# Second feed-forward of a fused decoder layer: a weight slot and two weight sums moved ahead of the last norms, the last rows' gain and bias moved from GpSimd to VectorE, and buffers of their own for two groups' sums

## What is computed

```python
x = _layernorm(ALPHA * x + m, ln2_g, ln2_b)                      # m: the mixer's output times w_out
x = _layernorm(ALPHA * x + 0.5 * _swiglu(x, w_gate, w_up, w_down), ln3_g, ln3_b)
```

## Time and profile before

| | us |
|---|---|
| median of 3 runs | 2378.47 |
| lowest, highest | 2376.24, 2378.83 |
| the profiled execution's own time | 2370.88 |
| its span, first to last instruction | 2368.3 |

### The profile page before, as it was taken

How to read it: one execution, slowest core, us unless ns; L and a number is a source line. 1 busy time by engine, 2 the same in 40 slices (tenths; PEclk the granted TensorE clock), 3 DMA queues, 4 the chain that set the end, 5 groups by cost and what they waited for, 6 DMA issues and landing times.

```text
span 2368.3 us, 52206 instructions
## 1 busy us (share of the span) xinstructions
PE 2281.4 (96%) x21030; PEld 2022.1 (85%) x21030; DVE 1563.6 (66%) x2616; ACT 1025.5 (43%) x1839; POOL 457.8 (19%) x452
## 2 busy tenths in 40 slices
PE   7999999999999999999998999997999999999997
PEld 7999999988888788856567898786999999998886
DVE  6776766665686756766644666747777766675577
ACT  6333333355454747544543353524433333345442
POOL 4222200001025102101110132446223300000105
PEclk9999999999999999999999999998999999999999
DMA  4465532378555444533332122434455533349652
GB/s 165 145 220 193 189 104 84 121 246 279 184 185 184 126 121 110 153 71 81 72 83 106 44 71 72 166 117 153 156 192 186 198 127 112 104 148 329 200 176 108
DMA packets 322577, 348.28 MB, mean 147 GB/s; under 512 B 49921, under 2 KB 220754, under 8 KB 321570
## 3 DMA queue, kind: packets, MB, share of 16 engines
q1 hardware_dynamic: 259650, 286.40, 38.1%
q10 hardware_dynamic: 60576, 53.65, 6.7%
q0 software_dynamic: 2112, 4.89, 0.8%
HBM read 245.91 MB, written 98.44 MB: 145 GB/s over the span
## 4 chain that ended last, share of the span: by engine, by line
PE 79%; DVE 9%; issue 5%; ACT 4%; DMA 1%; POOL 1%; SPq 1%; ACTq 0%; POOLq 0%; DVEq 0%
PE ps_b L763 19%; PE ps_a L763 18%; PE ps_a L470 7%; PE ps_b L470 6%; PE ps_pj L1541 4%; PE ps_rk L3253 4%; PE ps_wo L4075 4%; PE ps_mp L2306 2%; PE ps_pj L1523 2%; PE ps_mp L2334 2%; PE ps_rk L3349 1%; PE ps_mp L2320 1%; PE ps_rk L3263 1%; PE ps_mp L2288 1%; PE ps_rk L3401 1%
## 5 line engine op out<-in xcount | busy, mean ns | idle before, releaser
L763 PE MATMUL ps_b<-X_b,W_b 128*128 128x272 f32 x3696 | 466.7, 289 | 8.9 <-DVE X_b L1036 7.8
L763 PEld LDWEIGHTS ps_b<-X_b,W_b 128*128 128x128 f32 x3696 | 465.2, 189 | 10.3 <-DVE X_b L1036 8.0
L763 PE MATMUL ps_a<-X_a,W_a 128*128 128x272 f32 x3696 | 466.7, 289 | 5.6 <-DVE X_a L1036 2.4
L763 PEld LDWEIGHTS ps_a<-X_a,W_a 128*128 128x128 f32 x3696 | 464.9, 189 | 7.5 <-DVE G_a L1093 3.4
L470 PE MATMUL ps_b<-W_b,H_b 128*128 128x512 f32 x924 | 214.8, 389 | 1.0 <-DVE H_b L1122 1.0
L470 PE MATMUL ps_a<-W_a,H_a 128*128 128x512 f32 x924 | 215.3, 389 | 0.0
L470 PEld LDWEIGHTS ps_b<-W_b,H_b 128*128 128x128 f32 x924 | 173.3, 188 | 37.4 <-DVE W_b L1075 1.4
L470 PEld LDWEIGHTS ps_a<-W_a,H_a 128*128 128x128 f32 x924 | 173.2, 188 | 35.8
L844 ACT ACTIVATE W_b<-wraw_b 128x512 fp32r<-128x512 f32 x154 | 95.8, 629 | 164.2 <-PE ps_b L763 64.3
L844 ACT ACTIVATE W_a<-wraw_a 128x512 fp32r<-128x512 f32 x154 | 95.8, 629 | 164.0 <-PE ps_a L763 64.1
L1075 DVE TENSOR_TENSOR W_b<-wraw_b,W_b 128x512 fp32r<-128x512 f32 x154 | 118.5, 775 | 69.5 <-ACT W_b L844 69.5
(11 more groups left out here) (528 smaller groups left out, 4135.7 us busy)
## 6 DMA issues: line engine op xcount, KB each, us to landing
hraw_a<-hidden SPq DMA_DIRECT2D x77, 256.0 KB, 3.6
hraw_b<-hidden SPq DMA_DIRECT2D x77, 256.0 KB, 3.7
wraw_pj<-in_w_in SPq DMA_DIRECT2D x28, 512.0 KB, 3.7
wraw_a<-in_ffa_w_gate SPq DMA_DIRECT2D x22, 512.0 KB, 4.7
wraw_a<-in_ffa_w_up SPq DMA_DIRECT2D x22, 512.0 KB, 4.6
hraw_a<-in_ffa_w_down SPq DMA_DIRECT2D x22, 512.0 KB, 5.6
down_sums<-hraw_a SPq DMA_DIRECT2D x11, 1024.0 KB, 6.4
wraw_a<-down_sums SPq DMA_DIRECT2D x44, 256.0 KB, 2.9
```

Source lines behind the costliest of these rows:

```text
L763: last = nc.tensor.matmul(ps[:, bank + p, :PIECE], W[:, n % WC, wp, k * P:(k + 1) * P], operand(i, xp)[:, k, p * PIECE:(p + 1) * PIECE], s ...
```

## The change

- `out_projection` no longer emits the last `y_low`/`y_high` and the norms of tiles 7 and 8 itself; the feed-forward does, with its own work between them. On DVE the order becomes: low part of y's tile 8, `fill(0)`, `weight_sum(0, 0)`, `weight_sum(0, 1)`, norm of tile 7, gain of tile 7, norm of tile 8, items 0 to 4. On ACT: high part of y's tile 8, `fill(0)`, root and scaling of tile 7, then the items as before.
- Gain and bias of tile 8 are two DVE instructions on all 1024 columns (`last_gain`), put inside `x_parts(0)` ahead of its fifth instruction. POOL's L183 and L186 for tile 8 go, and POOL's first instruction of item 0 waits for them (`rows_normed`).
- Items 0 and 3 keep their sums in buffers of their own, `early` and `late`, which lie over weight slots 1, 2 and 3 to 5. So ACT's wait ahead of `first_parts(3)` goes, and ACT waits for POOL's item 0 ahead of `fill(1)` and for POOL's item 3 ahead of `fill(3)`. The weight sums no longer wait for POOL's item 0, and SP issues the third and fourth weight block behind POOL's item 1 in place of item 3.
- In the first feed-forward the buffers and waits change alike, and the order of the work stays.

```diff
-            t = (Z[:, j * P:], T[:, j, :], wraw[:, 2 + j // 2, j % 2 * 512:], hraw[:, j, :], wraw[:, 2 + j // 2, j % 2 * 512:])[q]
+            t = (Z[:, j * P:], early[:, j * 512:], wraw[:, 2 + j // 2, j % 2 * 512:], hraw[:, j, :], late[:, j * 512:])[q]
...
-            sp.wait_ge(Q.slo_made.h, Q.slo_made.at(16))
+            sp.wait_ge(Q.slo_made.h, Q.slo_made.at(8))
             for l in range(2, 4):
                 load_w(l)
...
-                if j == 3:
-                    act.wait_ge(Q.slo_made.h, Q.slo_made.at(4 * (j - 1)))
...
+                elif before is not None:
+                    before.rows_split(act)
+                if n in (1, 3):
+                    act.wait_ge(Q.slo_made.h, Q.slo_made.at(4 if n == 1 else 16))
                 copy(W[:, n % WC, 0, :], source(n)).then_inc(Q.w_hi.h, 1)
...
+            if before is not None:
+                before.last_rows_high(act)
+                fill(0)
+                before.norm_act(act)
             first_parts(0)
...
             def weight_sum(u, j):
-                if j == 0 and u == 0:
-                    dve.wait_ge(Q.slo_made.h, Q.slo_made.at(4))
-                elif j == 0:
+                if j == 0 and u > 0:
                     dve.wait_ge(Q.w_split.h, Q.w_split.at(7 * u))
...
+            if before is not None:
+                before.last_rows_low(dve)
+                fill(0)
+                weight_sum(0, 0)
+                weight_sum(0, 1)
+                before.norm_dve(dve, chain)
             for j in range(5):
-                x_parts(j)
-                if j == 0 and before is not None:
-                    before.last_gain(dve)
-                if j == 2:
+                x_parts(j, (lambda: before.last_gain(dve, chain)) if j == 0 and before is not None else None)
+                if j == 2 and before is None:
                     fill(0)
-            weight_sum(0, 0)
-            weight_sum(0, 1)
+            if before is None:
+                weight_sum(0, 0)
+                weight_sum(0, 1)
...
+            if before is not None:
+                before.rows_normed(pool)
             for n, q in enumerate(ITEMS):
...
-            for t in tiles:
+            for t in tiles[:-1]:
                 ln_pool(pool, chain, t)
...
+            def norm_dve(dve, chain):
+                ln_dve(dve, chain, NT - 2)
+                ln_dve(dve, chain, NT - 1, gain_first=True)
...
+        def rows_normed(self, pool):
+            pool.wait_ge(S.gained.h, S.gained.at(0))
+
+        def last_gain(self, dve, chain):
+            z = zt[:TS, (NT - 1) % ZS, :]
             dve.wait_ge(S.scaled.h, S.scaled.at(0))
-            nc.vector.tensor_tensor(z, z, gb[:TS, :D // 2], ALU.mult).then_inc(S.gained.h, 1)
+            nc.vector.tensor_tensor(z, z, gb[:TS, :], ALU.mult).then_inc(S.gained.h, 1)
+            dve.wait_ge(S.gained.h, S.gained.at(-1))
+            nc.vector.tensor_tensor(z, z, bb[:TS, :], ALU.add).then_inc(S.gained.h, 1)
```

More of the change, by code:

```diff
@@ L116, in layernorm_parts, with due @@
     xt, zt, stats, mv, std, gb, bb = bufs
+    closed = {}
+    def due(s, value):
+        return s.at(value - closed.get(s, 0))
     def sp_tile(sp, n):
@@ L132, in store, with dve_tile @@
         t = tiles[n]
[L133 removed]
+        if n < len(tiles) - 1:
+            sp.wait_ge(S.norm_made.h, due(S.norm_made, made))
+        else:
+            sp.wait_ge(S.gained.h, due(S.gained, n + 2))
         sp.dma_start(dst(t), zt[:rows_of(t), n % ZS, :]).then_inc(S.stored[n % ZS].h, 16)
     def late_store(sp, n):
[L138 removed]
+        store(sp, n, n + 1)
     def act_tile(act, n):
         r, s, z = rows_of(tiles[n]), n % 2, zt[:rows_of(tiles[n]), n % ZS, :]
[L142 removed]
+        act.wait_ge(S.var_made.h, due(S.var_made, n + 1))
         nc.scalar.activation(std[:r, s, 0:1], mv[:r, s, 1:2], ACT.Sqrt, bias=S.ln_eps[:r, :]).then_inc(S.std_made.h, 1)
[L144 removed]
+        act.wait_ge(S.scale_made.h, due(S.scale_made, n + 1))
         nc.scalar.activation(z, z, ACT.Identity, bias=std[:r, s, 1:2], scale=std[:r, s, 0:1]).then_inc(S.scaled.h, 1)
[L147 removed]
+    def dve_tile(dve, chain, n, gain_first=False):
         t = tiles[n]
@@ L190, in close @@
         for s in (S.z_made, S.var_made, S.std_made, S.scale_made, S.scaled, S.gained, S.norm_made):
-            s.close(n)
-        S.gb_in.close(32)
+            closed[s] = n
+        closed[S.gained], closed[S.norm_made], closed[S.gb_in] = n + 1, n - 1, 32
         for u in range(2):
-            S.res_in[u].close(16 * ((n + 1 - u) // 2))
+            closed[S.res_in[u]] = 16 * ((n + 1 - u) // 2)
         for u in range(ZS):
-            S.stored[u].close(16 * ((n + ZS - 1 - u) // ZS))
+            closed[S.stored[u]] = 16 * ((n + ZS - 1 - u) // ZS)
+        for s, total in closed.items():
+            s.close(total)
     return sp_tile, late_store, act_tile, dve_tile, pool_tile, close
@@ L341, in ffn @@
         sb("rest", [P, 256])
+        with ExitStack() as under:
+            under.enter_context(nc.sbuf_tensor(f"under_{tag}", [P, 1024], F32))
+            early = under.enter_context(nc.sbuf_tensor(f"early_{tag}", [P, 2048], F32))
+            under.enter_context(nc.sbuf_tensor(f"between_{tag}", [P, 704], F32))
+            late = under.enter_context(nc.sbuf_tensor(f"late_{tag}", [P, 2048], F32))
         W = sb("W", [P, WC, 2, 512], F32R)
@@ L1027, in _, with x_parts @@
             chain = Chain(S.dve_chain)
-            def x_parts(j):
+            def x_parts(j, between=None):
                 q = ITEMS[j]
@@ L1045, in x_parts @@
                 V.tensor_tensor(sums(q, 2), a11, sums(q, 2), ALU.subtract).then_inc(made.h, 1)
+                if between is not None:
+                    between()
                 low_part(0, a11)
@@ L4110, in _, with rows_high, norm_act @@
             ln_act(act, 0)
-            for t in tiles[2:]:
+            for t in tiles[2:-1]:
                 y_high(t)
                 ln_act(act, t - 1)
+            def rows_high(act):
+                y_high(NT - 1)
+            def norm_act(act):
+                ln_act(act, NT - 2)
+            last_step["high"], last_step["act"] = rows_high, norm_act
         @blk.vector
@@ L4143, in _, with rows_low @@
             ln_dve(dve, chain, 0)
-            for t in tiles[2:]:
+            for t in tiles[2:-1]:
                 y_low(t)
                 ln_dve(dve, chain, t - 1)
-            ln_dve(dve, chain, NT - 1)
+            def rows_low(dve):
+                y_low(NT - 1)
+            def norm_dve(dve, chain):
+                ln_dve(dve, chain, NT - 2)
+                ln_dve(dve, chain, NT - 1, gain_first=True)
+            last_step["low"], last_step["dve"] = rows_low, norm_dve
             S.dve_chain.close(chain.n)
```

41 lines of the change are left out of this document (27 added, 14 removed).

## The result

| | before | after |
|---|---|---|
| median of the runs of the comparison (19 of each) | 2376.46 us | 2382.17 us |
| the profiled execution | 2370.88 us, span 2368.3 | 2378.91 us, span 2376.9 |
| ratio of the times | | 1.0028, 95% interval 1.0019 to 1.0037 |

The change makes the kernel slower by 0.28%, 6.6 us by the ratio. The forecast was 4.8 us slower.

The account below looks back on a forecast made before the run. PE, busy for 96% of the span, was taken as the bound, so a later slot 1 moves the end one for one. Slot 1 4.8 us later, added to the median 2378.47, gave 2383.3 us, range 2378 to 2388.

Parts of the forecast that it names:

- The wait for the weights: DVE ahead of tile 7: weight blocks land at 1624.2 and 1625.6, so DVE is free for tile 7 at 1627.05.
- Tile 7's norm behind it: On DVE: tile 7's norm starts at 1627.05 in place of 1615.90, 11.15 later; ACT's scaling ends at 1632.1.
- The gain meets POOL: Tile 7's gain on DVE waits for one POOL instruction, ends at 1633.7; tile 8's product starts there, 10.3 later.
- Tile 8 to POOL's start: Item 0 starts at 1638.55; gain and bias on DVE take 2 x 1.21; POOL starts at 1643.55, 7.85 later.
- POOL's run to slot 1: Four POOL items of 4.94 end at 1663.3, two instructions of item 4 at 0.91 each end at 1665.1.
- Slot 0: PE's slot 0 starts at 1660.6, 5 us later, ends 1663.6 to 1665.5 beside POOL's run, costing nothing of its own.
- the first rival: VectorE loses the shared port repeatedly; fill(1) is kept back until POOL's run ends; 6 to 7 later, 2385; chance 0.22.
- What costs nothing: Stores, x loads, later weight blocks and ACT's new waits add nothing in the seam; first feed-forward late by tenths at most.
- The sum: Slot 1 starts at 1665.1 to 1665.6 against 1660.58, 4.6 to 5.0 later, 4.8 taken; 2383.3 in all.
- its last rival: The waits move but PE's slot 1 stays where it was, 2378.5; chance 0.03.
- the one in which the weights come in time: Blocks landed by 1615 let fill and sums fit DVE's idle time; slot 1 5.6 earlier, 2372.9; chance 0.08.
- the deciding point: Where faster turns to slower: tile 7's norm at about 1622.3 and the second weight block landing at 1620.9.

Follow-up runs that it names:

- the kernel with the earliest loads: Changed kernel with the first two weight blocks issued ahead of tile 7's and tile 8's residual loads; 2374.55 us, ratio to the kernel before 0.9979.
- POOL's wait: Changed kernel with POOL waiting for fill(1) ahead of item 4; one run, 2384.78 us.

## Why the prediction was right, and where not

Slower it was, by the mechanism that it gave. Its instants are on the clock of before; those of after have 4.06 taken off.

1. *The wait for the weights*: right. The second block landed at 1625.25 (forecast 1625.6), and DVE was free for tile 7 at 1626.67 (1627.05).
2. *Tile 7's norm behind it*: right, 10.77 later than in the earlier trace rows (11.15). The runs that let the blocks land earlier (two steps of it) or put the work behind the norms show that this wait is the cause.
3. *The gain meets POOL*: right in kind and size. The gain took 1.46, over the end of one POOL instruction, the bias of tile 6, and tile 8's product started at 1633.10 (1633.65).
4. *Tile 8 to POOL's start*: right. The two instructions on 64x1024 took 1.20 and 1.22 (1.21, the upper bound, was taken), and POOL started at 1642.91 (1643.55).
5. *POOL's run to slot 1*: mis-sized. Its instruction for slot 1 ended at 1663.57, not at 1665.1 to 1665.6. The sixteen took 19.8, as worked out. But the "two instructions of item 4 at 0.91 each" took 0.43 each: the row of before had been stretched by DVE's work beside it, and in after DVE did not get in, neither there nor among the sixteen.
6. *Slot 0*: right at 1660.09 (1660.6). The sentence that `fill(1)` "is ready on DVE at 1661.8 and has until 1665 to get past POOL" failed. It began at 1661.13, was kept back until POOL's run was over, and released slot 1 itself at 1665.08. This is what the first rival had said of this place. That slot 1 lies only 0.02 below the forecast's 1665.1 to 1665.6 is luck, two errors that meet: POOL 1.5 earlier than forecast, `fill(1)` 1.4 later than POOL.
7. *What costs nothing*: incomplete. On the clock of after, the late `fill(1)` delays the fills behind it, ACT's last one among them (1671.97), behind which ACT's first copy for the products stands (1672.50 to 1673.11). Slot 2 starts at 1673.20; it starts 0.09 to 0.10 behind the end of that copy in seven of the traces. Against before this is 1.05 later again. In this pair it cost nothing in the end, since the first blocks took it back, but no step had it.

The Trainium skill (SBUF — State Buffer, section "SBUF: two separate sides") has the engine that starts first keep the shared port pair for that whole instruction. By that alone a wait would end with the other engine's running instruction. The gain's 1.46 agrees. `fill(1)`'s 3.81 does not: POOL's instructions of that stretch are 1.3 at most and 0.43 at the end.

The sum, 4.8, against the profiled seam's 4.50 at slot 1 and 4.47 at the end, is right to 0.3. The runs give 6.6, with 4.5 to 8.8 as the interval. The difference to the traces stays open: the repeated execution of after ended its seam 5.59 later than before's first, and executions differ by up to 10 us ahead of the seam with unchanged code. The changed buffers of the first feed-forward show no cost of their own: its last product ended at 734.46 and 736.90 in the two traces of before, and at 734.07 to 738.81 in the nine with the change, which does not rule out one of 1 or 2 us.

The baseline has the clock in it, which no step has. Slot 1 of before did not wait for POOL, whose second instruction of item 4 ended at 1657.86, nor for `fill(1)`:

```profile
1658.23 1.00 DVE L1075 TENSOR_TENSOR W_b<-T_b,W_b 128x512 fp32r<-128x512 f32 x1 [0.70 <-ACT W_b L844]
```

That was ready at 1659.23, while PE was at slot 0 until 1660.58 at its lower clock. With slot 0 at 3.26, as in after, slot 1 of before might have begun 0.14 behind `fill(1)`, at 1659.4 (an estimate from these rows), and the change would have cost 5.7. The forecast took the measured 1660.58, so its sum is not touched, but "the trace's dependence of slot 1 on POOL", as it has it under its last rival, is not in the trace of before.

Of the rivals, the one in which the weights come in time is what the kernel with the earliest loads made: it put the second block before the deciding point, and the seam came out 5.22 earlier than before at slot 1 where 5.6 was worked out. That is close in spite of `fill(1)`, which held slot 1 back by 1.4 there as well.

## What to carry to other kernels

Before work is moved into an engine's idle time, look at when its data lands: here the gap lay from 1610.8 to 1615.9 and the blocks landed from 1624 on, so the wait took the gap's place and everything behind it slid. A move on one engine often needs a move on the queue that feeds it; with the load issued earlier the same change was 5 us faster than before and no longer slower. Most of that is not the move's: the kernel without the move was 3.67 faster in its trace, that with the early loads 5.11, and the 1.4 between them is hardly more than two executions of one kernel differ by. And a duration that was taken beside another engine's work is no price for the same instruction when that work has moved away, nor the other way round.

## What was not expected of the hardware

**A subtraction that waits for a whole run.** DVE's instructions on 128x512 with two inputs in SBUF take 0.64 to 0.69 alone. Beside POOL's back-to-back instructions some waited for one boundary (the gain's 1.46 beside POOL's bias, and 0.86 for `fill(0)` with the move undone beside low parts of 1.27) and some for many: 7.50 for `fill(0)` in both executions of before, at the same place to a few hundredths, and 3.81 to 4.50 for `fill(1)` in after, its repetition and three variants. Making POOL wait took `fill(1)` to 2.13, so it is POOL that keeps it back. What decides at which boundary DVE gets in stays open. It is not the moment within POOL's instruction alone: `fill(0)` with the move undone began 0.95 after the start of a POOL low part and got in behind it, and `fill(1)` in after began 0.94 after one and did not. That the long waits repeat to some hundredths from trace to trace speaks against chance.

**The clock inside the seam.** Slot 0 of before ran at 0.59, that of after at 1.00 with idle time of 1.73 in it, and slot 1 at 1.00 in after but at 0.66 with POOL's wait. A slot of the same 24 matmuls then takes 3.0 to 4.9 us, and 5.60 in the repetition of before. That difference is as large as most parts of this change are worth, so a single trace of a seam must be read with its granted clock beside it.
